# Two-block transformer on one core: the weight's high part takes x high and low in one 512-column matmul in the products of four and more blocks

## The reference

```python
def rms_norm(x, gain):
    xf = x.astype(jnp.float32)
    y = xf * lax.rsqrt(jnp.mean(xf * xf, axis=-1, keepdims=True) + EPS)
    return (y * gain.astype(jnp.float32)).astype(x.dtype)
...
def sqrelu_mlp(hn, w_up, w_down):
    return jnp.square(jax.nn.relu(hn @ w_up)) @ w_down
...
        h = h + hybrid_mixer(rms_norm(h, norm_mix[l]), w_in[l], lb_all[l], hgrn_onorm[l],
                             attn_qnorm[l], attn_knorm[l], w_out[l])
        h = h + memory_cross_attention(rms_norm(h, norm_cross[l]), rms_norm(mem, mem_norm[l]),
                                       wq_x[l], wk_x[l], wv_x[l], wo_x[l], xq_norm[l], xk_norm[l])
        h = h + sqrelu_mlp(rms_norm(h, norm_mlp[l]), w_up[l], w_down[l])
...
def pool_layer(x, mem, norm_g, w_in, w_pool, pool_scale, mem_g, w_mem_kv, w_out):
    ...
    return x + jnp.concatenate([y_pool, y_mem], axis=-1) @ w_out
```

## Time and profile before

| | us |
|---|---|
| median of three runs | 2660.87 (2658.78 to 2661.47) |
| the profiled execution | 2661.17, span 2659.4 |
| TensorE busy | 2442.1 (92%) |
| POOL busy | 1963.9 (74%) |
| ScalarE busy | 1057.7 (40%) |
| DVE busy | 983.0 (37%) |
| granted TensorE clock, mean | 0.948 of 2.4 GHz |

### The profile page before, as it was taken

One profiled execution on the slowest core, in us unless ns is written; L12 is line 12 of the kernel. 1 busy time (PEld: TensorE's weight loads), 2 busy tenths in 40 slices (PEclk: granted clock), 3 DMA queues, 4 the chain that ended last, 5 costly groups with the idle time before them and its releaser, 6 DMA issues.

```text
span 2659.4 us, 44622 instructions
## 1 busy us (share of the span) xinstructions
PE 2442.1 (92%) x18299; PEld 2337.5 (88%) x18299; DVE 983.0 (37%) x1484; ACT 1057.7 (40%) x1282; POOL 1963.9 (74%) x1380
## 2 busy tenths in 40 slices
PE   6999998878997899999999999998899967999996
PEld 6989997657896799999999999997899957988896
DVE  5026651635252353042041141605515043155522
ACT  3344444374334333333333333433434323245532
POOL 6888983655785679888898898788687858665572
PEclk8999998898998999999999999999999979889997
DMA  5654433433443345555555555564354535433241
GB/s 176 191 169 146 143 105 111 143 128 110 153 165 111 117 141 188 189 178 187 181 183 184 181 184 185 159 189 138 126 185 159 190 108 178 131 95 112 96 159 48
DMA packets 206436, 400.30 MB, mean 151 GB/s; under 512 B 10434, under 2 KB 20932, under 8 KB 205252
## 3 DMA queue, kind: packets, MB, share of 16 engines
q1 hardware_dynamic: 206276, 397.99, 46.2%
HBM read 395.87 MB, written 2.10 MB: 150 GB/s over the span
## 4 chain that ended last, share of the span: by engine, by line
PE 56%; POOL 24%; issue 9%; DVE 7%; ACT 2%; DMA 1%; POOLq 0%; SPq 0%; ACTq 0%; DVEq 0%
PE bank L579 49%; POOL w_low L546 24%; PE bank L696 1%; DVE x_high L1385 1%; DVE x_low L1389 1%; PE bank L779 1%; PE bank L715 1%; ACT w_high L1035 1%; PE bank L732 1%; DVE x_low L1473 0%; DVE x_high L1470 0%; PE bank L685 0%; DVE scratch L1398 0%; PE bank L670 0%; DVE heads_scratch L1802 0%
## 5 line engine op out<-in xcount | busy, mean ns | idle before, releaser
L546 POOL TENSOR_TENSOR w_low<-ring,w_high 128x256 fp32r<-128x256 f32 (+3 forms) x1312 | 1954.2, 1512 | 649.9 <-ACT w_high L1035 645.9
L1035 ACT ACTIVATE w_high<-ring 128x1024 fp32r<-128x1024 f32 (+2 forms) x760 | 786.9, 1039 | 1449.0 <-PE bank L579 1421.6
L579 PE MATMUL bank<-x_high,w_high 128*128 128x256 f32 x4196 | 1218.3, 290 | 72.5 <-issue 24.4
L579 PE MATMUL bank<-x_low,w_high 128*128 128x256 f32 x4196 | 1204.9, 287 | 0.0
L579 PE MATMUL bank<-x_high,w_low 128*128 128x256 f32 x4196 | 1204.2, 287 | 0.0
L579 PEld LDWEIGHTS bank<-x_high,w_high 128*128 128x128 f32 x4196 | 824.1, 196 | 85.1 <-issue 51.5
L579 PEld LDWEIGHTS bank<-x_low,w_high 128*128 128x128 f32 x4196 | 824.0, 196 | 1.6 <-issue 1.4
L579 PEld LDWEIGHTS bank<-x_high,w_low 128*128 128x128 f32 x4196 | 823.4, 196 | 0.0
L579 PE MATMUL bank<-hidden,w_high 128*128 128x256 f32 x2048 | 368.8, 283 | 0.0
L579 PEld LDWEIGHTS bank<-hidden,w_high 128*128 128x128 f32 x2048 | 319.5, 192 | 0.0
L579 PE MATMUL bank<-hidden,w_low 128*128 128x256 f32 x1024 | 289.8, 283 | 0.0
(11 more groups left out here) (250 smaller groups left out, 1727.7 us busy)
## 6 DMA issues: line engine op xcount, KB each, us to landing
ring<-in_w_in SPq DMA_DIRECT2D x64, 1024.0 KB, 5.5
ring<-in_w_up SPq DMA_DIRECT2D x64, 1024.0 KB, 5.4
ring<-in_w_down SPq DMA_DIRECT2D x64, 1024.0 KB, 5.0
ring<-in_w_out SPq DMA_DIRECT2D x48, 1024.0 KB, 5.0
ring<-in_a_w_in SPq DMA_DIRECT2D x32, 1024.0 KB, 5.4
ring<-in_b_w_in SPq DMA_DIRECT2D x32, 1024.0 KB, 5.3
ring<-in_w_kv SPq DMA_DIRECT2D x24, 1024.0 KB, 5.1
...
```

The lines of the kernel that those rows point to most:

```text
L546: last = pool.tensor_tensor(w_low[:, u % UNITS, part], ring[:, u // 2, first:first + n], w_high[:, u % UNITS, part], ALU.subtract)
L579: mm = pe.matmul(out, lhs, rhs, start=start and n == 0, stop=stop and n == 2, skip_group_check=True)
L1035: act.activation(w_high[:, u % UNITS, 0:n], ring[:, u // 2, r0 * g.width:r0 * g.width + n], ACT.Copy)\
```

## The change

`x_high` and `x_low` become two parts of one tensor `x_split` (tile, part, token), and so does `hidden`. The new `wide_unit` gives each weight tile one matmul of `w_high` with 512 columns (x high and low side by side) into a whole bank, and one of `w_low` with the 256 columns of x high into the bank's first half. A group thus takes four banks; groups alternate between banks 0 to 3 and 4 to 7. `wide_product` begins with a wait that all earlier groups have been read, and its second block waits for the norm's root, which reads bank 4. It serves hgrn_qf (4 blocks), mix_out (4), the eight MLP products (4 each), pool_in (6), out0 (4) and out1 (4).

DVE now has to add each bank's halves: `second_halves` copies the four second halves to scratch (or adds them to hT), a semaphore follows, `first_halves` adds the four first halves. In the up products scale and relu then run on the sum in SBUF, in `keep_wide` the scale does. ScalarE waits for the new `wide_kept` before the sigmoids of hgrn_qf and the silus of pool_in.

```diff
@@ -101,11 +101,11 @@
-        hidden = nc.alloc_sbuf_tensor_at("hidden", [P, 2, KT, T], F32R, offset=proj_at)
+        hidden = nc.alloc_sbuf_tensor_at("hidden", [P, KT, 2, T], F32R, offset=proj_at)
-        x_high = sb("x_high", [P, KT, T], F32R)
-        x_low = sb("x_low", [P, KT, T], F32R)
+        x_split = sb("x_split", [P, KT, 2, T], F32R)
+        x_high, x_low = x_split[:, :, 0, :], x_split[:, :, 1, :]
...
@@ -594,6 +596,21 @@
+            def wide_unit(g, b, u, four, x, first, of, more=0):
+                pe.wait_ge(low_ready, 8 * b + u + 1 + more)
+                wh, wl = parts(u, g)
+                r0, rows = g.unit(u)
+                for k in range(rows):
+                    kt = first + r0 + k
+                    for f in range(4):
+                        cols = slice(f * P, f * P + P)
+                        pe.matmul(four[f][:, :], wh[:, k, cols], x(kt), start=(kt == 0), stop=False,
+                                  skip_group_check=True)
+                        mm = pe.matmul(four[f][:, 0:T], wl[:, k, cols], x(kt)[:, 0:T], start=False,
+                                       stop=(kt == of - 1), skip_group_check=True)
+                mm.then_inc(units_used, 1)
...
@@ -611,6 +628,28 @@
+            def wide_product(name, x, made, ready=x_ready, sums=None):
+                g = PLAN[name]
+                pe.wait_ge(evacuated, g.g0)
+                def block_of(n, more, more_groups, wait):
+                    group_free(g.g0 + n, more_groups)
+                    for u in range(8):
+                        if wait and u == 6 and sums:
+                            sums()
+                        if wait and u % 2 == 0:
+                            pe.wait_ge(ready, made + u // 2 + 1)
+                        wide_unit(g, g.b0 + n, u, bank[4 * (n % 2):4 * (n % 2) + 4], x, 4 * (u // 2), KT, more)
+                for n in range(2):
+                    if n == 1 and sums:
+                        pe.wait_ge(norm_root, normed[0])
+                    block_of(n, 0, 0, n == 0)
+                with pe.Fori(0, g.blocks // 2 - 1) as i:
+                    for q in range(2):
+                        block_of(2 + q, i * 16, i * 2, False)
...
@@ -765,7 +805,7 @@
-            product("hgrn_qf", features_unit, operand, made=x_made["mix"], sums=norm_sum)
+            wide_product("hgrn_qf", operand_parts, x_made["mix"], sums=norm_sum)
...
@@ -884,7 +924,7 @@
-            product("mix_out", features_unit, operand, made=x_made["mix_y"])
+            wide_product("mix_out", operand_parts, x_made["mix_y"])
...
@@ -902,11 +942,11 @@
-                product(f"up{part}", features_unit, operand, made=x_made["mlp"] if part == 0 else None, sums=norm_sum)
-                product(f"down{part}", features_unit, hidden_tile, made=4 * part + 1, ready=hidden_ready)
-            product("pool_in", features_unit, operand, made=x_made["pool"], sums=norm_sum)
+                wide_product(f"up{part}", operand_parts, x_made["mlp"], sums=None if part else norm_sum)
+                wide_product(f"down{part}", hidden_parts, 4 * part + 1, ready=hidden_ready)
+            wide_product("pool_in", operand_parts, x_made["pool"], sums=norm_sum)
...
@@ -918,7 +958,7 @@
-            product("out0", features_unit, operand, made=x_made["pool_y"])
+            wide_product("out0", operand_parts, x_made["pool_y"])
...
@@ -995,7 +1035,7 @@
-            product("out1", features_unit, operand, made=x_made["nsa_y"])
+            wide_product("out1", operand_parts, x_made["nsa_y"])
...
@@ -1157,7 +1197,7 @@
-            act.wait_ge(evacuated, PLAN["hgrn_v"].g0)
+            act.wait_ge(wide_kept, 4)
...
@@ -1229,7 +1269,7 @@
-            act.wait_ge(evacuated, PLAN["pool_qm"].g0)
+            act.wait_ge(wide_kept, 10)
...
@@ -1333,27 +1376,77 @@
+            halves_done, wide_keeps = [0], [0]
+            def second_halves(four, read, out=None):
+                for f in range(4):
+                    b = four[f][:, T:2 * T]
+                    if out is None:
+                        last = dve.tensor_copy(second[:, f * T:f * T + T], b)
+                    else:
+                        last = dve.tensor_tensor(out(f), b, out(f), ALU.add)
+                last.then_inc(halves_read, 1)
+                dve.wait_ge(halves_read, read)
+            def first_halves(four, out=None):
+                for f in range(4):
+                    to = second[:, f * T:f * T + T] if out is None else out(f)
+                    last = dve.tensor_tensor(to, four[f][:, 0:T], to, ALU.add)
+                return last
+            def wide_groups(name, body):
+                g, read = PLAN[name], halves_done[0]
+                dve.wait_ge(evacuated, g.g0)
+                with dve.Fori(0, g.groups // 2) as i:
+                    for q in range(2):
+                        dve.wait_ge(units_used, i * (2 * g.units) + g.made(q))
+                        body(i, q, bank[4 * q:4 * q + 4], i * 2 + (read + q + 1))
+                halves_done[0] += g.groups
+            def keep_wide(name, t0):
+                g = PLAN[name]
+                def body(i, q, four, read):
+                    second_halves(four, read)
+                    first_halves(four).then_inc(evacuated, 1)
+                    dve.wait_ge(evacuated, i * 2 + (g.g0 + q + 1))
+                    dve.tensor_tensor(proj[:, bass.ds(i * 8 + (t0 + 4 * q), 4), :],
+                                      second.rearrange("p (a t) -> p a t", a=4), scale_four, ALU.mult)\
+                       .then_inc(wide_kept, 1)
+                    dve.wait_ge(wide_kept, i * 2 + (kept + q + 1))
+                kept = wide_keeps[0]
+                wide_groups(name, body)
+                wide_keeps[0] += g.groups
+            def residual(name):
+                def body(i, q, four, read):
+                    h = lambda f: hT[:, bass.ds(i * 8 + (4 * q + f), 1), :].rearrange("p a t -> p (a t)")
+                    second_halves(four, read, h)
+                    first_halves(four, h).then_inc(evacuated, 1)
+                wide_groups(name, body)
-                for c in range(2):
-                    h = hT[:, 4 * j + 2 * c:4 * j + 2 * c + 2, :].rearrange("p a t -> p (a t)")
-                    last = dve.tensor_tensor(h, bank[2 * ((g.g0 + j) % 2) + c][:, :], h, ALU.add)
+                if name == "cross_out":
+                    for c in range(2):
+                        h = flat(hT, 4 * j + 2 * c, 2)
+                        last = dve.tensor_tensor(h, bank[2 * ((g.g0 + j) % 2) + c][:, :], h, ALU.add)
+                else:
+                    halves_done[0] += 1
+                    four = bank[4 * (j % 2):4 * (j % 2) + 4]
+                    h = lambda f: hT[:, 4 * j + f, :]
+                    second_halves(four, halves_done[0], h)
+                    last = first_halves(four, h)
-            def residual(name):
-                g = PLAN[name]
-                dve.wait_ge(evacuated, g.g0)
-                with dve.Fori(0, 2) as i:
-                    for q in range(2):
-                        n = g.g0 + q
-                        dve.wait_ge(units_used, i * (2 * g.units) + g.made(q))
-                        for c in range(2):
-                            h = hT[:, bass.ds(i * 8 + (4 * q + 2 * c), 2), :].rearrange("p a t -> p (a t)")
-                            last = dve.tensor_tensor(h, bank[2 * (n % 2) + c][:, :], h, ALU.add)
-                        last.then_inc(evacuated, 1)
...
@@ -1574,7 +1669,7 @@
-            keep("hgrn_qf", scaled_tiles(0))
+            keep_wide("hgrn_qf", 0)
...
@@ -1754,30 +1849,28 @@
-            squares = heads_scratch[:, 0:1024]
-                with dve.Fori(0, 2) as i:
-                    for q in range(2):
-                        n = g.g0 + q
-                        dve.wait_ge(hidden_ready, i * 2 + (4 * part + q + 1))
-                        dve.wait_ge(units_used, i * (2 * g.units) + g.made(q))
-                        for c in range(2):
-                            last = dve.scalar_tensor_tensor(
-                                out=squares[:, c * 512:c * 512 + 512].rearrange("p (a t) -> p a t", a=2),
-                                in0=two(bank[2 * (n % 2) + c]), scalar=0.0, in1=scale_two, op0=ALU.max, op1=ALU.mult)
-                        last.then_inc(evacuated, 1)
-                        dve.wait_ge(evacuated, i * 2 + (n + 1))
-                        dve.tensor_tensor(squares, squares, squares, ALU.mult).then_inc(hidden_squared, 1)
-                        dve.wait_ge(hidden_squared, i * 4 + (8 * part + 2 * q + 1))
-                        high, low = (hidden[:, c, bass.ds(i * 8 + 4 * q, 4), :].rearrange("p a t -> p (a t)")
-                                     for c in range(2))
-                        dve.tensor_copy(high, squares).then_inc(hidden_squared, 1)
-                        dve.wait_ge(hidden_squared, i * 4 + (8 * part + 2 * q + 2))
-                        dve.tensor_tensor(low, squares, high, ALU.subtract).then_inc(hidden_ready, 1)
```

(18 more changed lines are left out.)

24 lines of the change are left out of this document (16 added, 8 removed).

## The result

The changed kernel takes **2684.19 us** (median of 4 runs, 2681.54 to 2688.58) against 2660.68 (2658.78 to 2661.47) of the kernel before on the same chip: ratio 1.0093, 95% interval 1.008 to 1.0106, slower by 23.5 us. The forecast was 2680 in 2666 to 2697. The profiled execution took 2684.84 us, its span is 2683.1.

The account below looks back on a forecast made before the run. TensorE was taken to set the pace inside products, with waits for VectorE outside them. Added waits, read-outs and low clock of 64.1 us less 45.6 saved by the pairs give +18.5 on 2661.2: 2680 us, range 2666 to 2697.

Parts of the forecast that it names:

- Part 1, the pairs: Wide products: 512 plus 256 columns replace three matmuls of 256, 13.2 ns less per weight tile, 3456 tiles: -45.6 us.
- D: Rival: the change doesn't quicken the matmuls, the gain is zero and the time 2725 us; chance 0.03.
- Seven joints: Between MLP up and down products TensorE stands 3.3 us at each, waiting for the last group's read-out: +23.1 us.
- The clock behind them: After each of the seven MLP stops the granted clock falls, losing 1.6 us each: +11.2 us.
- B: Rival, dearer joints: low clock twice as long, read-out 3.5 us, or POOL slowed by DVE: 2684 to 2703 us; chance 0.14.
- A: Rival: the clock holds at the seven MLP joints, so without the 11.2 us the time is 2668.5 us; chance 0.14.
- cross_out to up0: up0 now waits for cross_out's group 3, which DVE reads after the operand quarters and folds: +9.4 us.
- down3 to pool_in: TensorE stands 12.5 us before pool_in's first matmul, while the later stop at its fifth unit goes: +9.2 us.
- mix_out to cross_q, out0 to cmp_kv: The next product's fifth unit waits on group 3 through ScalarE's squares; both stops grow 2 us each: +4.0 us.
- pool_in to the pooling: Pooled sums wait for the longer last read-out plus a scaling pass through SBUF of 2.6 us: +4.6 us (3.9 to 5.3).
- Norms: Second group of hgrn_qf, up0 and pool_in: a faster TensorE meets the wait for the root 0.3 us sooner: +0.9 us.
- C: Rival: the waits are not on the path, the seven stops and their clock vanish: 2645 us, faster; chance 0.07.

Follow-up runs that it names:

- The direct measurement: Changed kernel with its banks, waits and read-outs, but three matmuls of 256 columns per weight tile instead of one of 512 and one of 256: 2712.78 us.
- the order four by four: Four 512-column matmuls, then four of 256, instead of alternating: 2680.95 us in the changed kernel; 2640.77 us with the superfluous wait removed and cross_out's group read first.
- the kernel before with the wait: Kernel before, plus a wait until every earlier group is read at the start of seven MLP products (down0 to down3, up1 to up3): 2673.66 us.
- the read ahead of the folds: Best version (wait removed, cross_out read first, four wide then four narrow) with mix_out's, down3's and out0's last group read before VectorE's two folds: 2640.36 us.

## Why the prediction was right

Its verdict and its mechanism hold, and its time is 4 us off; two errors of opposite sign lie in that, so the near hit of the time is partly luck. The pairs save 17 us less than forecast, and by that alone the time would have been 2697, the edge of the range; everything else adds up to 12 us less than forecast, 3.3 of them a difference between the two executions. Point by point, from the profiled executions, whose spans differ by 23.7 us:

- *Part 1, the pairs.* Forecast -45.6. At the paces of the trace 12 groups save 13.3 ns and 42 save 6.7 ns a pair: 64 x (12 x 13.3 + 42 x 6.7) = -28.2. This is the term that was mis-sized, by 17. The step that failed is "226.8 + 120.0": two prices from streams of one width were added and taken to hold everywhere in a stream that alternates. The sum, 346.8, is the short level, and 42 of the 54 groups have 353.3. D's price, zero, was wrong further off. The direct measurement says 28.6. Of the rule from the Trainium skill (TensorE: Matmul & The Clock Gate, "Wait — 56ns, not 53.3ns?"), about 2.5 ns for a warm matmul, the estimate was 8.6 us: these runs don't agree with it. A matmul less is worth 6.7 to 13.3 ns here, and 9.2 in the order four by four.
- *Seven joints.* Forecast 3.3 us each, 23.1; measured 3.05 and 3.08, 21.5. The read-out was put at 3.0 and is 2.9.
- *The clock behind them.* Forecast 1.6 us at all seven, 11.2. It fell at five. A product with a fall takes 95.33 us from start to start, four groups of 22.61 and a stop of 3.08 account for 93.5, which leaves 1.8; with the few tenths that a product without a fall has left over as well, 1.5 to 1.6 are the clock's, some 8 in all. In the four kernels that keep these stops it fell at 17 of 28, and at three of the 17 it stayed low for 6.8 us in place of 3.4, as B feared for all. So A (it holds) was wrong as an all-or-nothing case; each joint decides for itself.
- *cross_out to up0.* 9.4 forecast; up0 starts 15.19 us after the last matmul in place of 5.75, 9.4. *down3 to pool_in.* 12.5 forecast, 12.26 measured, and the fifth unit's stop behind it is gone, as said.
- *mix_out to cross_q, out0 to cmp_kv.* 4.0 forecast; the stops are 6.08 and 4.93 where 3.20 and 3.18 were: 4.6.
- *pool_in to the pooling.* 4.6 forecast; from the last read to the first pooled copy it is 3.5 more (4.83 us against 1.32), as the scaling pass takes 1.60 us and not 2.6. The 1.92 that the forecast read as a pass with POOL away stands beside a POOL that was at work (957.13 on, in the trace of before). And TensorE gets only 1.1 us of the 3.5: the pooled sums that follow take 30.9 us where they took 33.4, with two of their copies at 0.17 us each in place of 2.11 and 2.33, beside a POOL that is idle there for 5.10 us in place of 2.81. *The end.* 1.7 forecast; 1.6. *Norms.* 0.9 forecast; TensorE stands for 0.06 to 0.17 us ahead of the three second groups, 0.4.

The terms measured come to 21.5 + 8 + 9.4 + 9.1 + 4.6 + 3.5 + 1.6 - 28.2 = 29.5. Six of that are missing in the 23.7. The pooling's 2.4 are the first part. Another 3.3 are in the attention ahead of out1, 184.7 us in the trace of before and 181.4 in that of after, and the clock accounts for them: in the first it fell once more. Before and after, at the same place of the attention:

```profile
2382.00:2388.00 6.00, 6.00 (x25) 5.02 (x24) 0.91 (x8) 1.06 (x5) 0.18 (x1) 0.50 0.07 25
...
2411.00:2417.00 6.00, 6.00 (x48) 5.81 (x48) 2.31 (x9) 2.92 (x9) 1.65 (x3) 1.00 0.01 3
```

The five profiles with such a fall of 6.8 us there have 184.7 to 185.0 us, three of them of wide kernels; the six without it have 181.4 to 181.7, the kernel before with the wait among them. So it is a difference between executions, not the change's. What is left is small in sum, but single stretches still differ by more than their terms: from the start to mix_out after is 3.0 us shorter where its pairs give 1.7, and behind out1's start 1.6 shorter where pairs and read-out give 0.1. Those stay open.

B's dear read-out (3.5 us) didn't come. That POOL works without a gap beside DVE did, for 28 units of 2.72 us in up0 and for 8 and then 16 in up3, but TensorE waited for it for 0.23 us only there. C lost: without the waits the kernel is 34 us faster, so they are on the path.

The version that beats both kernels is the changed one without its superfluous wait, with cross_out's group read first and matmuls four by four: 2640.77 us, 0.7% below the kernel before (2640.36 with the read ahead of the folds, no different). The step from three matmuls to two was sound. What made it a loss was a wait that guarded banks which were already free, and a read in DVE's order that a bank layout had turned into a start condition.
